# Placing the quads' weight sums in the FFN stages by the order in which the first 26-product body fills its buffers

## The reference

```
def conv_ffn(x, w_in, conv_w, conv_b, w_out):       # second block: approximate gelu, centred convolution
    h = causal_dwconv(x @ w_in, conv_w, conv_b)     # w_in: 1024 x 5632, three taps
    gate, val = h[..., :D_FF], h[..., D_FF:]        # D_FF = 2816
    return (jax.nn.gelu(gate) * val) @ w_out        # w_out: 2816 x 1024
```

## Time and profile before

| what | value |
|---|---|
| median of 3 runs | 3266.47 us (3266.37 to 3276.89) |
| the profiled execution | 3274.88 us, its span 3273.2 us |
| TensorE busy | 3189.1 us (97%) |
| VectorE busy | 1902.6 us (58%) |
| GpSimd busy | 1548.7 us (47%) |
| ScalarE busy | 1076.3 us (33%) |
| mean granted TensorE clock | 0.991 |

### The profile page before, as it was taken

One profiled execution on the slowest core, in us unless ns is written; L12 is line 12 of the kernel. 1 busy time (PEld: TensorE's weight loads), 2 busy tenths in 40 slices (PEclk: granted clock), 3 DMA queues, 4 the chain that ended last, 5 costly groups with the idle time before them and its releaser, 6 DMA issues.

```text
span 3273.2 us, 49903 instructions
## 1 busy us (share of the span) xinstructions
PE 3189.1 (97%) x16674; PEld 2564.1 (78%) x16674; DVE 1902.6 (58%) x3860; ACT 1076.3 (33%) x2383; POOL 1548.7 (47%) x1383
## 2 busy tenths in 40 slices
PE   8999999999999999999999999999999999999998
PEld 7787888867777788886446888868888688778887
DVE  6676667455555566746446555466663634476754
ACT  3533333123332233313326343123331334223322
POOL 4343887323221388742001444448873431468843
PEclk9999999999999999999999999999999999999999
DMA  3223222211111222221210111222222111222231
GB/s 137 79 84 123 78 85 103 81 56 59 59 52 39 97 78 96 91 97 46 70 46 27 65 58 58 78 78 93 96 97 77 66 58 65 78 78 84 97 103 52
DMA packets 68767, 250.60 MB, mean 77 GB/s; under 512 B 7568, under 2 KB 7568, under 8 KB 68544
## 3 DMA queue, kind: packets, MB, share of 16 engines
q1 hardware_dynamic: 68544, 247.72, 21.8%
HBM read 245.59 MB, written 2.10 MB: 76 GB/s over the span
## 4 chain that ended last, share of the span: by engine, by line
PE 90%; DVE 4%; ACT 2%; issue 2%; POOL 1%; DMA 0%; DVEq 0%; SPq 0%; ACTq 0%; POOLq 0%
PE psum L2665 28%; PE psum L2711 27%; PE psum L774 6%; PE psum L2602 5%; PE psum L2896 4%; PE psum L2193 3%; PE psum L1726 3%; PE psum L1753 2%; PE psum L2218 1%; PE psum L806 1%; PE psum L2908 1%; PE psum L1780 1%; PE psum L844 1%; ACT scratch L1440 1%; PE psum L828 1%
## 5 line engine op out<-in xcount | busy, mean ns | idle before, releaser
L3766 POOL TENSOR_TENSOR scratch<-scratch 128x512 f32<-128x512 f32 (+1 forms) x440 | 467.6, 1073 | 152.0 <-PE psum L2711 82.6
L2665 PE MATMUL psum<-scratch 128*128 128x256 f32 (+2 forms) x2080 | 511.9, 384 | 13.0 <-issue 13.0
L2665 PEld LDWEIGHTS psum<-scratch 128*128 128x128 f32 x2080 | 397.6, 191 | 74.2 <-issue 14.5
L3506 DVE TENSOR_TENSOR scratch<-scratch,psum 128x256 f32<-128x256 f32 (+2 forms) x720 | 299.5, 422 | 226.8 <-PE psum L2665 208.1
L2711 PE MATMUL psum<-scratch 128*128 128x256 f32 (+2 forms) x1856 | 414.3, 381 | 0.2
L2711 PEld LDWEIGHTS psum<-scratch 128*128 128x128 f32 x1856 | 352.3, 190 | 52.2 <-issue 1.6
L3474 DVE SCALAR_TENSOR_TENSOR psum<-scratch,params,psum 128x256 f32<-128x256 f32 (+2 forms) x704 | 312.4, 485 | 50.3 <-ACT psum L3082 50.3
L2984 ACT ACTIVATE scratch<-psum 128x256 f32<-128x256 f32 (+2 forms) x216 | 82.5, 385 | 555.2 <-PE psum L2711 532.1
L3706 POOL TENSOR_TENSOR scratch<-w_ring 128x512 f32<-128x512 f32 (+2 forms) x56 | 69.8, 1246 | 404.2 <-PE psum L2711 194.5
L3102 ACT ACTIVATE scratch<-psum 128x256 f32<-128x256 f32 (+2 forms) x320 | 123.3, 385 | 418.3 <-PE psum L2665 414.6
L2711 PE MATMUL psum<-acts,scratch 128*128 128x256 f32 (+2 forms) x976 | 223.2, 384 | 4.9 <-DVE stream L3338 3.8
(11 more groups left out here) (541 smaller groups left out, 5997.1 us busy)
## 6 DMA issues: line engine op xcount, KB each, us to landing
w_ring<-units SPq DMA_DIRECT2D x335, 512.0 KB, 3.5
scratch<-units SPq DMA_DIRECT2D x128, 512.0 KB, 4.3
residual<-x_t SPq DMA_DIRECT2D x4, 528.0 KB, 6.4
out_t<-residual SPq DMA_DIRECT2D x2, 512.0 KB, 3.4
out_t<-residual SPq DMA_DIRECT2D x1, 768.0 KB, 4.4
params<-cols SPq DMA_DIRECT2D x1, 568.5 KB, 11.1
out_t<-residual SPq DMA_DIRECT2D x1, 256.0 KB, 3.3
gate_w_sb<-gate_w SPq DMA_DIRECT2D x1, 96.0 KB, 10.6
```

The source lines that it names most:

```text
L2665: mm = nc.tensor.matmul(PS[:, bank, 0:H], weights(q), moving(q), start=(opens and q == 0), stop=(q == 1), skip_group_check=True)
L3506: v.tensor_tensor(row, row, PS[:, rank_bank(j, at), 0:H], ALU.add if sign > 0 else ALU.subtract).then_inc(r_later, 1)
L3766: g.tensor_tensor(blocks([RANK_BUFFERS + o for o, _, _ in sums]), blocks([a for _, a, _ in sums]), blocks([e for _, _, e in sums]), ALU.ad ...
```

## The change

SUM_PLACE is no longer fixed. It is filled from RANK_SUMS: the places in the order in which the first 26-product body first writes a buffer of them (2, 7, 4, 1, 5, 6, 0, 3) are given to the weight sums in the order in which the quads' products use them: (2, 0), (2, 1), (3, 0), (3, 1), (1, 0), (1, 1), (4, 0), (4, 1). GpSimd's first 26-product body gets one more wait, for all eight weight sums of the quads' body, in front of its first instruction. The last four moving sums are made in reversed order, and the products that use them name the new numbers.

```
@@ RANK_PRODUCTS
-    (29, 16, ('v', 19, 0), 3, False),
+    (29, 16, ('v', 16, 0), 3, False),
...
-    (8, 0, ('v', 18, 0), 5, False),
+    (8, 0, ('v', 17, 0), 5, False),
...
-    (6, 0, ('v', 17, 0), 4, True),
-    (17, 6, ('v', 16, 0), 'turns', False),
+    (6, 0, ('v', 18, 0), 4, True),
+    (17, 6, ('v', 19, 0), 'turns', False),
@@ RANK_MOVING
+    ('sub', ('v', 13, 0), ('v', 15, 0)),
+    ('neg', ('x', 0, 1), ('x', 1, 1)),
+    ('sub', ('x', 1, 1), ('x', 2, 1)),
     ('sub', ('v', 5, 0), ('v', 1, 0)),
-    ('sub', ('x', 1, 1), ('x', 2, 1)),
-    ('neg', ('x', 0, 1), ('x', 1, 1)),
-    ('sub', ('v', 13, 0), ('v', 15, 0)),
@@
-        SUM_PLACE = {(n, q): 2 * (2, 3, 1, 4).index(n) + q for n in (1, 2, 3, 4) for q in range(2)}
+        SUM_PLACE = {}
+        for _, sums, _, _ in RANK_SUMS:
+            for buffer, _, _ in sums:
+                if buffer // 2 not in SUM_PLACE.values():
+                    SUM_PLACE[(2, 3, 1, 4)[len(SUM_PLACE) // 2], len(SUM_PLACE) % 2] = buffer // 2
@@ rank_weights
+                if j == 1:
+                    pool.wait_ge(q_weight, weight_ready(0, b, 4, 1))
                 for at, (op, sums, ready, left) in enumerate(RANK_SUMS):
```

## The result

The changed kernel takes 3281.23 us (median of 14 runs, 3277.91 to 3287.62), the kernel before 3270.76 (14 runs, 3266.37 to 3276.89): ratio 1.003, 95% interval 1.0022 to 1.0038. It is 10.5 us slower, and measurably so, though within the 0.5% that I had named as the limit. The profiled execution has a span of 3280.7 us against 3273.2. As in the prediction, the threes are the products (3, 0) and (3, 1) of the quads' body, the sixth product is that of the first 26-product body.

The account below looks back on a forecast made before the run. TensorE, 97% busy, bounds the kernel; each FFN stage's loss goes from 7.8 us to 10.2 to 13.5 (idles 4.0 and 3.0, clock 3.2 plus 0 or 3.3). Four stages, +15 on 3266.47, give 3281.5; range 3258 to 3294.

Parts of the forecast that it names:

- The sums' start: First FFN stage: GpSimd's first three sums for the 26-product body would start at 307.7, 309.5 and 316.6 us.
- The four moving sums' order: VectorE's queue: reversing the last four moving sums costs 0, since their first consumer is the 17th product.
- The new wait: GpSimd's wait on all eight quad sums before its first 26-product sum costs nothing, as they were long done.
- VectorE's delay: First FFN stage: GpSimd's sums set VectorE's moving sums back 4.8 us, quad sum 22 moving from 316.88 to 321.7.
- the idle before the threes: Quads' body: TensorE idles 4.0 us before products (3, 0) and (3, 1), waiting for VectorE's late quad sum.
- the lock: Two-SBUF-input VectorE and SBUF-reading GpSimd instructions exclude each other; a 512-wide sum sets VectorE back 1.10 us, a 256-wide 0.53.
- The sixth product: First 26-product body: 3.0 us idle before product 6, which could start at 330.1 but waits for VectorE until 333.1.
- The clock: FFN stages: half clock after the 4.0 us idle, 3.2; possibly a second stretch, 3.3, in one or two of four.
- within 0.5%: Outcome class: a difference from the kernel before of at most 16.3 us either way; chance 0.57.
- B: VectorE's moving sums keep pace, GpSimd gives way; only product 6's idle remains; -19 to -6 us, 3247 to 3260; chance 0.15.
- C: Gains and new waits cancel: delay before the threes 2 to 3 us; -7 to +5, 3260 to 3272; chance 0.14.
- D: Change does not act: a load or the wait holds GpSimd's sums until the threes are done; 3266; chance 0.03.

Follow-up runs that it names:

- The filled idles: Changed kernel with nine filler matmuls before the threes and six before the sixth product: 3270.95 us, ratio 1.0001 to the kernel before.
- the sums held: Changed kernel with GpSimd's first sum of the 26-product bodies waiting until VectorE has made moving sum 15: 3257.57 us, ratio 0.9961 to the kernel before.
- only written: Changed kernel with GpSimd's first five sums of each stage replaced by memsets that read nothing: 3259.67 us, ratio 0.9958 to the kernel before.
- the run with both moves: Changed kernel, VectorE's quad sums 22 queued before moving sums 12 to 15, last four moving sums behind additions of products 9, 12, 17, 18: 3246.72 us, ratio 0.992.

## Why the prediction was right

The forecast was 3281.5 with a stage 2.4 to 5.7 us slower; the stages came out 2.3, 2.9, 2.7 and 3.1 slower, the median 3281.23. The mechanism was right; the clock was over-priced, and that the medians agree within 0.3 us is in part luck.

- **The sums' start.** Forecast 307.7, 309.5 and 316.6 for the first three; measured 307.26, 309.04 and 316.13 in a stage that runs 0.5 ahead. The four moving sums' order: 0, as forecast (the run with the order alone: 1.0003). The new wait: 0, by the start of the first sum.
- **VectorE's delay.** 4.8 forecast, 4.2 + 0.5 = 4.7 measured; the idle before the threes 4.0 forecast, 3.8 to 4.0 measured. That the lock is the cause is shown twice, by holding GpSimd back and by taking its reads away.
- **The sixth product.** 3.0 forecast, 2.8 measured; removed by moving the last four moving sums, enlarged to 4.5 by moving four others in front of it. The body itself started at 328.06, not at 325.7: the half clock, which the forecast priced apart, fell on the threes (6.57 us instead of 3.72) and delayed VectorE's next work by the same amount.
- **The clock.** This is the term that was mis-sized. I priced one low stretch at 3.2 us and gave one or two stages of four a second one at 3.3. In fact three of four stages had a second one, but both were then short, and together they cost 3.2 us by the busy time in them, where one long one costs 2.7 to 2.8. The filled idles give the same price, 3.2 us a stage. The idles were also 0.3 shorter a stage than forecast (6.7 instead of 7.0). So the sum came out at its lower end, 10.9 instead of 15. The median agrees with the forecast better than its working does: I added 15 to the 3266.47 of the first three runs, and 14 runs put the kernel before at 3270.76, 4.3 higher. The two errors, 4.1 too much and 4.3 too little, cancel by luck.
- **The chances.** 10.5 us is 0.32% and lies in "within 0.5%", the likeliest case. Rivals B, C and D are out: the moving sums lost their turns as in the earlier trace rows, the idle before the threes was 3.9, and GpSimd did start early.

What stays open: why the low stretches after nearly equal idles (3.8 to 4.0 us) were long in the first stage and short in the others. In the run with the places alone it was the other way round for the first stage (two short ones), so it is no property of a stage.

## What to carry to other kernels

Work moved into another engine's idle time is not free when a third engine is in the middle of a stream of two-input SBUF operations: price the overlap by a place in the trace where the two already meet. When an engine becomes early, list what its neighbour must deliver next and put that first in the neighbour's queue; here the same change cost 11 us with the old order of VectorE's queue and saved 22 with a new one. And an addition of work to a queue shows up at the next product that needs that queue, so removing one idle alone may only move it.

## What was not expected of the hardware

The half clock had two lengths after idles of the same kind: before the change 6.8 us after each of four idles of 3.2 to 3.3, after it 6.7 once and 3.3 to 3.4 six times after idles of 2.8 to 4.0. Nor does an idle of this size always bring it: with the sums held or only written, one idle of 2.6 to 2.9 us was left in each stage, and the clock stayed at 1.00 around it in the fourth stage (2870 to 2892 and 2865 to 2897).

The spread of the times does not go away with the low stretches of these bodies: the kernel before spreads over 10.5 us in 14 runs (3266.37 to 3276.89), and the run with both moves, which has none in the two stages shown, over 8.3 in 6 (3242.98 to 3251.31). What sets it, no run here tests.
